# Spreading rows of norm scales by two small DMAs through memory instead of by matmuls, in a two-model float32 transformer kernel

## The chip, the cores and the metric

The kernel runs on one core of one Trainium2 chip, as one program of five engines that meet only at semaphores: TensorE (PE: matmuls and, beside them, weight loads), VectorE (DVE), ScalarE (ACT), GpSimd (POOL) and SyncE (SP, which issues most loads). 16 DMA engines move data between the chip's memory (HBM) and the on-chip SBUF. The metric is the device time of one run in microseconds (us), as the median of three runs.

## The reference

256 tokens of width 1024 go through three layers. Layer 0 has a mixer of sparse attention and pooling, layer 1 one of stick-breaking attention, layer 2 (a second model) one of retention and block-sparse attention; each mixer is followed by a feed-forward block (FFN). All is float32. Every mixer and every FFN starts with a norm of the rows, and this case is about what becomes of the rows' scales:

```python
def rms_norm(x, g):
    y = x32 * lax.rsqrt(jnp.mean(x32 * x32, axis=-1, keepdims=True) + EPS)
    return (y * g.astype(jnp.float32)).astype(x.dtype)

def swiglu(h, w1, w3, w2):
    return (jax.nn.silu(h @ w1) * (h @ w3)) @ w2

for layer in range(DEPTH):
    h = rms_norm(x, norm_mix_g[layer])
    x = x + mixer(h)
    h = rms_norm(x, norm_ffn_g[layer])
    x = x + swiglu(h, ffn_w1[layer], ffn_w3[layer], ffn_w2[layer])
```

## The kernel before

**Numbers.** Each float32 operand is split into a high part that PE takes as it is and a low part that holds the rest (ACT makes `high`, a subtraction on DVE makes `low`: lines 849/1399 for weights in the ring `raw`, 854/1405 for sums of weights in `arena`). A product takes three matmuls, high by high, high by low, low by high (L2149, L2150, L2154). PE is thus given a long, even row of matmuls, a unit of weights at a time, and DVE and ACT work some units ahead of it.

**Where scales go.** The x that PE multiplies (`xh`, `xl`) carries the norm's gain but not the row's scale: token p and token 128+p lie in partition p as `r0` and `r1` (`x_rstd(k, 0)`, `x_rstd(k, 1)`; k is the norm's number), and the products are scaled afterwards. POOL makes the scales in `row_rstd` (L764 and the power at L767), norm by norm, as the rows of x are finished.

**Who needs a row of them.** Some of the FFN's up-products, and the two gate products of layer 2's mixer, are made with seven products in place of eight, from sums of quarters of x and of the weights. These sums mix tokens p and 128+p, so the first half of x must first be brought to the second half's scale, by the ratio r0/r1 (`x_ratio`). x is transposed there, tokens along the free axis, so the 128 ratios are needed as a row, the same in all 128 partitions. Layer 1's mixer wants its q and k transposed and scaled by a row of all 256 scales. There are five such rows: norms 1, 3, 6 (the FFNs, f = 0, 1, 2), norm 4 (`mx_...`) and norm 2 (`o_rstd`).

**How PE spreads them.** DVE makes a matrix of ones, the reciprocal of r1, the ratio, and a diagonal matrix of the ratios (L1636 to L1641; L1936 to L1941 for norm 4; L1902 and L1904 for norm 2). PE multiplies ones by diagonal into a PSUM bank (`x_row_scales` L2389, L2873, `norm_rows` L2660; a float32 matmul shows as two pieces). In the FFN and the gates DVE reads that bank in the product of `x_sums` (L1594; L1947 for norm 4); for norm 2 ACT copies it to `o_rstd` (L1256), which `qk_scale` reads (L1913).

**Order.** Every engine's order is written out by hand. In an FFN, PE does two units of chunk 0, the small matmul, two units of chunk 1 with `hiddenT(0)` between them (transposes L2293, which wait for DVE's `gated(0, ...)`, L1540), `down(0)`, and then the first pair of seven products. DVE does the split of unit (1, 1), `x_sums` (L1594 to L1603), `gated(0, 1)`, `gated(0, 0)`, the first sum of weights (L1573), and goes on splitting. POOL, behind the scales of a norm, issues the load of the next norm's gains (`load_gain`, L753; after norm 1 first a table, L816), and in an FFN later four accumulating loads of weights (`weight_sums`, L798).

## Time and profile before

| | before |
|---|---|
| median of 3 runs | 951.77 us (951.42 to 952.23) |
| profiled execution: span from the first to the last instruction | 949.9 us |
| PE matmul busy | 942.9 us, 99% of the span |
| DVE / ACT / POOL busy | 795.1 / 578.5 / 80.7 us |
| granted TensorE clock | 1.00 throughout |

The span leaves out what lies around the instructions; the median is 1.9 us longer. Busy shares are means over the whole span: the page's table of 40 slices shows DVE at nine tenths or more in most slices of the three FFNs, and at five to eight tenths in many of those between them, while PE is at nine tenths or more in all but the first and the last.

### The profile page before, as it was taken

To read this page: it belongs to the slowest core of one execution; us is meant where nothing else is said; L and a number is where in the kernel's file an instruction comes from. 1 tells how busy PE (TensorE), PEld (TensorE's weight loads), DVE (VectorE), ACT (ScalarE), POOL (GpSimd) and SP (SyncE) were. 2 spreads that over 40 slices of the span, in tenths; PEclk is the share of its full clock that TensorE was granted. 3 is DMA by queue.
4 is the path that set the end of the run, shared out by engine and by line. 5 is a ranking of instruction groups with operands and counts; after the bars stand their busy time and mean duration, and the time that the engine had idled before them with its cause. 6 is when DMAs were issued, how large, how long until landed. Compare 5 with 4: busy or idle time off the path is not lost.

```text
span 949.9 us, 12049 instructions
## 1 busy us (share of the span) xinstructions
PE 942.9 (99%) x4719; PEld 786.6 (83%) x4719; DVE 795.1 (84%) x827; ACT 578.5 (61%) x611; POOL 80.7 (8%) x87
## 2 busy tenths in 40 slices
PE   8999999999999999999999999999999999999998
PEld 7878888888899888888888888888888888888887
DVE  5988999989866877999989887965885779999996
ACT  6566676576663655676666666565744456665672
POOL 3511101101000000101101021001010001101010
PEclk9999999999999999999999999999999999999999
DMA  8746888785464436879786365457255485987751
GB/s 303 263 134 210 245 305 226 203 284 133 153 223 136 155 112 220 244 252 258 199 280 163 116 219 182 171 182 218 93 198 196 164 275 139 318 236 208 256 133 45
DMA packets 125849, 191.14 MB, mean 201 GB/s; under 512 B 7256, under 2 KB 87520, under 8 KB 125792
## 3 DMA queue, kind: packets, MB, share of 16 engines
q1 hardware_dynamic: 110992, 172.59, 53.9%
q0 software_dynamic: 14496, 17.57, 10.5%
q8 instruction: 38, 0.62, 0.3%
q10 hardware_dynamic: 304, 0.20, 0.1%
q14 instruction: 19, 0.16, 0.0%
HBM read 189.29 MB, written 1.05 MB: 200 GB/s over the span
## 4 chain that ended last, share of the span: by engine, by line
PE 99%; DMA 0%; ACT 0%; issue 0%; DVE 0%; ACTq 0%
PE psum L2149 27%; PE psum L2150 26%; PE psum L2154 26%; PE psum L2293 4%; PE psum L2142 2%; PE psum L2144 2%; PE psum L2143 2%; PE psum L2684 1%; PE psum L2695 1%; PE psum L2685 1%; PE psum L2310 1%; PE psum L2718 1%; PE psum L2334 1%; PE psum L2746 1%; PE psum L2493 0%; DMA gains<-in_norm_mix_g 0%
## 5 line engine op out<-in xcount | busy, mean ns | idle before, releaser
L1399 DVE TENSOR_TENSOR low<-raw,high 128x2048 fp32r<-128x2048 f32 (+1 forms) x109 | 245.3, 2252 | 60.1 <-ACT high L849 60.1
L849 ACT ACTIVATE high<-raw 128x2048 fp32r<-128x2048 f32 (+1 forms) x112 | 211.6, 1890 | 83.8 <-PE psum L2154 69.1
L2149 PE MATMUL psum<-high,xh 128*128 128x512 f32 x596 | 237.1, 398 | 0.0
L2150 PE MATMUL psum<-high,xl 128*128 128x512 f32 x596 | 232.6, 390 | 0.0
L854 ACT ACTIVATE high<-arena 128x2048 fp32r<-128x2048 f32 x88 | 168.7, 1917 | 76.3 <-PE psum L2154 72.1
L1405 DVE TENSOR_TENSOR low<-arena,high 128x2048 fp32r<-128x2048 f32 x88 | 200.5, 2284 | 11.1 <-ACT high L854 11.1
L2154 PE MATMUL psum<-low,xh 128*128 128x512 f32 x596 | 155.4, 390 | 0.0
L2149 PEld LDWEIGHTS psum<-high,xh 128*128 128x128 f32 x596 | 112.0, 188 | 23.3 <-issue 0.7
L2154 PEld LDWEIGHTS psum<-low,xh 128*128 128x128 f32 x596 | 111.7, 188 | 23.6 <-issue 0.3
L2150 PEld LDWEIGHTS psum<-high,xl 128*128 128x128 f32 x596 | 112.0, 188 | 22.0
L2149 PE MATMUL psum<-high,mh 128*128 128x512 f32 x256 | 102.1, 399 | 0.0
L2150 PE MATMUL psum<-high,ml 128*128 128x512 f32 x256 | 99.9, 390 | 0.0
L2149 PE MATMUL psum<-high,gh 128*128 128x512 f32 x248 | 96.8, 390 | 0.0
L2150 PE MATMUL psum<-high,gl 128*128 128x512 f32 x248 | 96.5, 389 | 0.0
L2154 PE MATMUL psum<-low,mh 128*128 128x512 f32 x256 | 67.4, 389 | 0.0
L2154 PE MATMUL psum<-low,gh 128*128 128x512 f32 x248 | 61.5, 389 | 0.0
L2154 PEld LDWEIGHTS psum<-low,mh 128*128 128x128 f32 x256 | 48.1, 188 | 10.2
L2149 PEld LDWEIGHTS psum<-high,mh 128*128 128x128 f32 x256 | 48.1, 188 | 9.9 <-issue 0.3
L2150 PEld LDWEIGHTS psum<-high,ml 128*128 128x128 f32 x256 | 48.1, 188 | 9.4
L2154 PEld LDWEIGHTS psum<-low,gh 128*128 128x128 f32 x248 | 46.6, 188 | 9.7
L2149 PEld LDWEIGHTS psum<-high,gh 128*128 128x128 f32 x248 | 46.6, 188 | 9.6
L2150 PEld LDWEIGHTS psum<-high,gl 128*128 128x128 f32 x248 | 46.6, 188 | 9.6
(252 smaller groups left out, 1183.8 us busy)
## 6 DMA issues: line engine op xcount, KB each, us to landing
raw<-in_ffn_w SPq DMA_DIRECT2D x68, 512.0 KB, 6.5
arena<-in_ffn_w SPq DMA_DIRECT2D x64, 512.0 KB, 7.5
raw<-in_w_in SPq DMA_DIRECT2D x50, 512.0 KB, 4.6
raw<-in_od_w_qkv SPq DMA_DIRECT2D x24, 512.0 KB, 4.6
raw<-in_w_ffn_down SPq DMA_DIRECT2D x22, 512.0 KB, 6.4
arena<-in_ffn_w POOLq DMA_DIRECT2D x16, 512.0 KB, 7.5
arena<-in_w_ffn_gate SPq DMA_DIRECT2D x16, 512.0 KB, 6.5
arena<-in_w_ffn_up SPq DMA_DIRECT2D x16, 512.0 KB, 8.2
```

The lines of the kernel that those rows point to most:

```text
L849: nc.scalar.activation(high[:, n % RING, 0:cols], raw[:, r, 0:cols], ACT.Copy).then_inc(high_ready, 1)
L854: nc.scalar.activation(high[:, n % RING, :], src, ACT.Copy).then_inc(high_ready, 1)
L1399: nc.vector.tensor_tensor(low[:, n % RING, 0:cols], raw[:, RING_AT[n] % RING, 0:cols], high[:, n % RING, 0:cols].bitcast(F32), ALU.subtrac ...
L1405: nc.vector.tensor_tensor(low[:, n % RING, :], src, high[:, n % RING, :].bitcast(F32), ALU.subtract).then_inc(low_ready, 1)
L2142: nc.tensor.matmul(out, sh, wh, start=start, stop=False, skip_group_check=True)
L2143: nc.tensor.matmul(out, sh, wl, start=False, stop=False, skip_group_check=True)
L2144: return nc.tensor.matmul(out, sl, wh, start=False, stop=stop, skip_group_check=True)
L2149: nc.tensor.matmul(out, sh, wh, start=start, stop=False, skip_group_check=True)
L2150: nc.tensor.matmul(out, sl, wh, start=False, stop=False, skip_group_check=True)
L2154: return nc.tensor.matmul(out, sh, slot_tile(low, n, k, cols)[:, c0:c1], start=False, stop=stop, skip_group_check=True)
L2293: ins = nc.tensor.transpose(bank(dst_bank, j * P, (j + 1) * P), src, ident)
L2310: ins = nc.tensor.matmul(bank(lb[e], c0, c1), qT[rows, t * P:(t + 1) * P], kT[rows, 0:c1 - c0], start=t == 1, stop=masked and t == 0, skip ...
```

## The change

The row is no longer made by PE. POOL makes the ratio itself (`ratio_row`: the square root of the mean square by a power of 0.5, then r0 times that), issues a DMA that stores the 128 ratios (for norm 2 the 256 scales) as one line of a new tensor `rows_out` in the chip's memory, waits until it has landed, and issues a second DMA that loads this line into all 128 partitions (`spread_row`). DVE's `x_sums` reads the row from SBUF and waits for the second DMA (`ratio_row_in`, `rstd_row_in`) instead of for PE. The small matmuls, the ones, the diagonals, DVE's reciprocal and ratio, ACT's copy, and the waits that kept the PSUM banks free for them, are gone. POOL's loads of gains and of the table now stand behind the two small DMAs. The core of the diff:

```diff
+        rows_out = nc.dram_tensor("rows_out", (len(NORMS), SEQ), F32, kind="Internal").ap()
@@ POOL
+            nc.gpsimd.memset(pos_half, 0.5).then_inc(half_ready, 1)
+            def spread_row(k, src, dst, done):
+
+                i = ROW_NORMS.index(k)
+                row = rows_out[i, 0:src.shape[1] * P]
+                with nc.allow_non_contiguous_dma(reason="one value of each partition"):
+                    pool.dma_start(row.rearrange("(t p) -> p t", p=P), src).then_inc(row_stored, 16)
+                pool.wait_ge(row_stored, 16 * (i + 1))
+                pool.dma_start(dst, row.partition_broadcast(P)).then_inc(done, 16)
+
+            def ratio_row(k, dst):
+
+                nc.gpsimd.tensor_tensor(x_inv, msq[:, 2 * k + 1:2 * k + 2], pos_half, ALU.pow).then_inc(inv_made, 1)
+                pool.wait_ge(inv_made, ratio_seq(k))
+                pool.wait_ge(rstd_ready, 2 * NORMS.index(k) + 1)
+                nc.gpsimd.tensor_tensor(x_ratio, x_rstd(k, 0), x_inv, ALU.mult).then_inc(ratio_ready, 1)
+                pool.wait_ge(ratio_ready, ratio_seq(k))
+                spread_row(k, x_ratio, dst, ratio_row_in)
             for e in (1, 2, 3, 4):
                 row_rstd(e, e)
+                if e == 2:
+                    pool.wait_ge(rstd_ready, 6)
+                    spread_row(2, rstd[:, 4:6], o_rstd, rstd_row_in)
+                else:
+                    ratio_row(e, m_ratio if e == 4 else f_ratio)
@@ DVE, x_sums of an FFN
-                    dve.wait_ge(rbc_ready, f + 1)
+                    dve.wait_ge(ratio_row_in, 16 * ratio_seq(FFN_NORM[f]))
-                    nc.vector.tensor_tensor(f_x[:, :, 0:P], f_x[:, :, 0:P], bank(7, 0, P).unsqueeze(1).to_broadcast([P, KD, P]), ALU.mult
+                    nc.vector.tensor_tensor(f_x[:, :, 0:P], f_x[:, :, 0:P], f_ratio.unsqueeze(1).to_broadcast([P, KD, P]), ALU.mult
-                nc.vector.memset(f_ones, 1.0).then_inc(prep_step, 1)
-                nc.vector.reciprocal(x_inv, r1).then_inc(prep_step, 1)
-                nc.vector.tensor_tensor(x_ratio, r0, x_inv, ALU.mult).then_inc(prep_step, 1)
-                nc.vector.tensor_scalar(f_diag, ident, x_ratio, None, ALU.mult).then_inc(diag_ready, 1)
@@ PE, an FFN
-                x_row_scales()
+                pe.wait_ge(x_copied, 4 * f + 4)
@@ PE, layer 1's mixer
-                if u == 2:
-                    norm_rows()
@@ PE, layer 2's mixer
-                    nc.tensor.matmul(bank(5, 0, P), m_ones, m_diag, start=True, stop=True, skip_group_check=True).then_inc(mx_rbc, 1)
-                    if f == 0:
-                        pe.wait_ge(mx_step, 4)
```

On POOL, at the first FFN, the rows before run from the second scale of norm 1 to the table, the gains and the first accumulating load:

```order
L764 TENSOR_SCALAR small<-small 128x1 [waits sumsq_ready]
L767 TENSOR_TENSOR small<-small 128x1 [waits msq_ready]
L816 DMA cst<-consts 128x1536 [waits pooled_ready]
L753 DMA gains<-in_norm_mix_g 128x1024 [waits xn_ready]
L798 DMA arena<-in_ffn_w 128x4x256 [waits t_ready]
```

The same stretch of POOL in the changed kernel, where L774 and L777 are the scale, L791 and L794 the root and the ratio, L785 the store and L787 the load:

```order
L774 TENSOR_SCALAR small<-small 128x1 [waits sumsq_ready]
L777 TENSOR_TENSOR small<-small 128x1 [waits msq_ready]
L791 TENSOR_TENSOR small<-small 128x1
L794 TENSOR_TENSOR small<-small 128x1 [waits rstd_ready,inv_made]
L785 DMA rows_out<-small 128x1 [waits ratio_ready]
L787 DMA arena<-rows_out 128x128 [waits row_stored]
L849 DMA cst<-consts 128x1536 [waits pooled_ready]
L762 DMA gains<-in_norm_mix_g 128x1024 [waits xn_ready]
L826 DMA arena<-in_ffn_w 128x4x256 [waits t_ready]
```

Four rows came in between scale and table, two of them DMAs, and the load waits on POOL for the store. FFN 1 and FFN 2 read alike, without the table, and FFN 2 without the gains.

On DVE, in the first FFN, the rows before go from a split to `x_sums` and the two `gated` (L1399 are splits):

```order
L1399 TENSOR_TENSOR low<-raw,high 128x2048 [waits high_ready]
L1636 MEMSET arena 128x128 [waits rstd_ready]
L1637 RECIPROCAL small<-small 128x1
L1639 TENSOR_TENSOR small<-small 128x1 [waits prep_step]
L1641 TENSOR_SCALAR arena<-cst,small 128x128 [waits prep_step]
L1399 TENSOR_TENSOR low<-raw,high 128x2048 [waits high_ready]
L1594 TENSOR_TENSOR arena<-arena,psum 128x8x128 [waits x_copied,rbc_ready]
```

The same stretch of DVE in the changed kernel (L1431 are the splits, L1626 is the product of `x_sums`, L1572 the two `gated`):

```order
L1431 TENSOR_TENSOR low<-raw,high 128x2048 [waits high_ready]
L1431 TENSOR_TENSOR low<-raw,high 128x2048 [waits high_ready,rstd_ready]
L1626 TENSOR_TENSOR arena<-arena 128x8x128 [waits x_copied,ratio_row_in]
L1630 TENSOR_TENSOR arena<-arena 128x4x128 [waits prep_step]
L1631 TENSOR_TENSOR arena<-arena 128x4x128
L1633 TENSOR_TENSOR arena<-arena 128x4x128 [waits prep_step]
L1635 TENSOR_TENSOR arena<-arena 128x4x128 [waits prep_step]
L1572 SCALAR_TENSOR_TENSOR arena<-psum,small,arena 128x256 [waits silu_ready] x2
```

Four small instructions are gone ahead of the second split; the product of `x_sums` keeps its place and waits for the DMA's row.

## Rows read from the trace of the kernel before

**Rows 1.** The page: busy time by engine, and its chain by engine.

```profile
PE 942.9 (99%) x4719; PEld 786.6 (83%) x4719; DVE 795.1 (84%) x827; ACT 578.5 (61%) x611; POOL 80.7 (8%) x87
PE 99%; DMA 0%; ACT 0%; issue 0%; DVE 0%; ACTq 0%
```

**Rows 2.** All waits of PE: engine, line, releaser: us, times, longest.

```profile
PE psum L2499 <- DMA gains<-in_norm_mix_g: 4.2, 1, 4.2
```

**Rows 3.** Timeline of PE, first FFN: start us, us, engine, line, operation, tiles, count.

```profile
99.09 0.38 PE L2389 MATMUL psum<-arena 128*128 128x128 f32 x2
99.23 0.48 PE L2149 MATMUL psum<-high,xh 128*128 128x512 f32 x1
99.54 0.40 PE L2150 MATMUL psum<-high,xl 128*128 128x512 f32 x1
99.78 0.40 PE L2149 MATMUL psum<-high,xh 128*128 128x512 f32 x1
```

**Rows 4.** All pieces of L2389 and of L2873: ns min/median/max, first and last start.

```profile
L2389 PE MATMUL psum<-arena x6: 270/272/273, 99.1 to 783.7; 128*128 128x128 f32 x6
L2873 PE MATMUL psum<-arena x2: 270/272/273, 563.5 to 563.7; 128*128 128x128 f32 x2
```

**Rows 5.** Timeline of PE, layer 1's mixer, the row of norm 2.

```profile
275.18 0.60 PE L2660 MATMUL psum<-arena 128*128 128x128 f32 x4
275.54 0.36 PE L2684 MATMUL psum<-xh,high 128*128 128x256 f32 x1
275.74 0.28 PE L2685 MATMUL psum<-xl,high 128*128 128x256 f32 x1
275.86 0.28 PE L2684 MATMUL psum<-xh,high 128*128 128x256 f32 x1
```

**Rows 6.** Timeline of POOL, first FFN: the second scale of norm 1.

```profile
89.88 0.56 POOL L767 TENSOR_TENSOR small<-small 128x1 f32<-128x1 f32 x1
```

**Rows 7.** Timeline of DVE, first FFN: two splits, `x_sums`, the two `gated`.

```profile
89.98 2.28 DVE L1399 TENSOR_TENSOR low<-raw,high 128x2048 fp32r<-128x2048 f32 x1
...
92.78 2.28 DVE L1399 TENSOR_TENSOR low<-raw,high 128x2048 fp32r<-128x2048 f32 x1
...
99.51 1.22 DVE L1594 TENSOR_TENSOR arena<-arena,psum 128x1024 f32<-128x1024 f32 x1
...
103.43 0.87 DVE L1540 SCALAR_TENSOR_TENSOR arena<-psum,small,arena 128x256 f32<-128x256 f32 x2
```

**Rows 8.** Timeline of PE, first FFN: `hiddenT(0)`.

```profile
104.81 0.60 PE L2293 MATMUL psum<-cst,arena 128*128 128x128 f32 x4
```

**Rows 9.** Timeline of POOL, layer 2's mixer: an instruction alone and beside a split.

```profile
693.99 0.19 POOL L829 TENSOR_SCALAR small<-small 128x4 f32<-128x4 f32 x1 [39.19 <-DVE small L1983]
694.27 1.03 POOL L832 TENSOR_TENSOR small<-small 128x4 f32<-128x4 f32 x1
695.56 2.14 POOL L829 TENSOR_SCALAR small<-small 128x4 f32<-128x4 f32 x1 [0.27 <-DVE small L1983]
```

**Rows 10.** Timeline of DVE in the same stretch: the split.

```profile
695.39 2.26 DVE L1399 TENSOR_TENSOR low<-raw,high 128x2048 fp32r<-128x2048 f32 x1
```

**Rows 11.** Landing of POOL's gains load issued at 378.75 us (512 KB, L753).

```profile
DMA to landing us min/median/max: 3.9/3.9/3.9
```

**Rows 12.** Landing of POOL's eight loads of 0.2 KB near the start (L781).

```profile
DMA to landing us min/median/max: 5.1/5.7/5.8
```

**Rows 13.** Issues of the output's stores: engine, count, KB each, us to landing.

```profile
out<-xs SPq DMA_DIRECT2D x3, 256.0 KB, 2.0
```

**Rows 14.** A stretch of the first FFN: busy by engine, clock, DMA share, GB/s.

```profile
95.00:99.00 4.00, 4.00 (x19) 3.33 (x18) 2.45 (x6) 1.92 (x1) 0.00 (x0) 1.00 1.01 398
```

**Rows 15.** Timeline of DVE: first readers of norm 2's and of norm 4's row.

```profile
287.14 0.68 DVE L1913 TENSOR_TENSOR arena<-psum,arena 128x512 f32<-128x512 f32 x1
...
569.80 1.21 DVE L1947 TENSOR_TENSOR arena<-arena,psum 128x1024 f32<-128x1024 f32 x1
```

**Rows 16.** Timeline of POOL in layer 2's mixer: its next work behind norm 4.

```profile
564.01 3.30 POOL L774 TENSOR_TENSOR head_rs<-small 128x8 f32<-128x8 f32 x2 [8.56 <-DVE small L1485]
```

More of the change, by code:

```diff
@@ L287, in program @@
         gn_rstd = small[:, 238:246].rearrange("p (t h) -> p t h", t=NT)
+        pos_half = small[:, 190:191]
         x_ratio, x_inv = small[:, 254:255], small[:, 255:256]
@@ L320, in program @@
         f_s1 = take(512)
-        f_diag = take(P)
-        f_ones = take(P)
+        f_ratio = take(P)
         f_x = XT2.rearrange("p (k n) -> p k n", k=KD)
@@ L348, in program @@
         o_tok = blocks(take(NT * 512), NT)
-        o_ones, o_diag, o_rstd = take(P), blocks(take(SEQ), NT), take(SEQ)
+        o_rstd = take(SEQ)
         take.at = 4 * 512
@@ L372, in program @@
         r_kT = gate_b[:, 1, :].rearrange("p (j t) -> p j t", j=4)
-        m_ones, m_diag = arena[:, take.at:take.at + P], arena[:, take.at + P:take.at + 2 * P]
+        m_ratio = arena[:, take.at:take.at + P]
         r_v = blocks(take(NT * D), NT)
@@ L411, in program @@
         x_copied = sem("x_copied")
-        t_ready, t3_in, prep_step, rbc_ready = sem("t_ready"), sem("t3_in"), sem("prep_step"), sem("rbc_ready")
-        diag_ready = sem("diag_ready")
+        t_ready, t3_in, prep_step = sem("t_ready"), sem("t3_in"), sem("prep_step")
+        inv_made, ratio_ready = sem("inv_made"), sem("ratio_ready")
+        row_stored, ratio_row_in, rstd_row_in = sem("row_stored"), sem("ratio_row_in"), sem("rstd_row_in")
         sums_high, sums_low = sem("sums_high"), sem("sums_low")
@@ L556, in p2_unit, with ratio_seq @@
             return U_P2[0] + j + (3 if j >= 2 * P2_PAIR + 4 else 0)
+        RATIO_NORMS = (1, 3, 4, 6)
+        ROW_NORMS = sorted(RATIO_NORMS + (2,))
+        def ratio_seq(k):
+            return RATIO_NORMS.index(k) + 1
         def b12_block(p):
@@ L834, in _ @@
             row_rstd(6, 5)
+            ratio_row(6, f_ratio)
             weight_sums(2)
@@ L1253, in _ @@
                 chunk_half(1)
-                if u == 2:
-                    act.wait_ge(rbc_made, 1)
-                    nc.scalar.activation(o_rstd, bank(RBC_BANK, 0, SEQ), ACT.Copy).then_inc(rbc_copied, 1)
                 if u == Q_T_BEFORE:
@@ L1900, in _ @@
             nc.vector.memset(o_later.rearrange("p e (b n) -> p e b n", n=P)[:, :, 0:TRI // P:2, P - 1], 1.0).then_inc(ones_set, 1)
-            dve.wait_ge(rstd_ready, 6)
-            nc.vector.memset(o_ones, 1.0).then_inc(rdiag_ready, 1)
-            for t in range(NT):
-                nc.vector.tensor_scalar(o_diag[:, t, :], ident, x_rstd(2, t), None, ALU.mult).then_inc(rdiag_ready, 1)
             def qk_scale(half, f):
@@ L1935, in _ @@
             r0, r1 = x_rstd(4, 0), x_rstd(4, 1)
[L1936 to L1941 removed]
             def mx_sums():
[L1945 removed]
+                dve.wait_ge(ratio_row_in, 16 * ratio_seq(4))
                 dve.wait_ge(mx_copied, 4)
[L1947 removed]
+                nc.vector.tensor_tensor(m_x[:, :, 0:P], m_x[:, :, 0:P], m_ratio.unsqueeze(1).to_broadcast([P, KD, P]), ALU.mult
                                         ).then_inc(mx_step, 1)
                 a11, a12, a21, a22 = (m_x[:, 4 * q:4 * q + 4, t * P:(t + 1) * P] for t in range(NT) for q in range(2))
[L1950 removed]
+                dve.wait_ge(mx_step, 1)
                 nc.vector.tensor_tensor(a22, a21, a22, ALU.subtract).then_inc(mx_step, 1)
                 nc.vector.tensor_tensor(a21, a21, a11, ALU.subtract).then_inc(mx_step, 1)
[L1953 removed]
+                dve.wait_ge(mx_step, 3)
                 nc.vector.tensor_tensor(a11, a11, a22, ALU.subtract).then_inc(mx_step, 1)
[L1955 removed]
+                dve.wait_ge(mx_step, 4)
                 nc.vector.tensor_tensor(a12, a12, a11, ALU.subtract).then_inc(mx_step, 1)
@@ L2383, in sum_tile @@
                     return tile
-                def x_row_scales():
-                    pe.wait_ge(diag_ready, f + 1)
-                    pe.wait_ge(x_copied, 4 * f + 4)
-                    nc.tensor.matmul(bank(7, 0, P), f_ones, f_diag, start=True, stop=True,
-                                     skip_group_check=True).then_inc(rbc_ready, 1)
                 def product_1(p):
@@ L2654, in q_T @@
                     transposes(Q_T_BANK + t, [o_tok[:, t, j * P:(j + 1) * P] for j in range(4)], qkvT_ready)
-            def norm_rows():
-                pe.wait_ge(rdiag_ready, 1 + NT)
-                for t in range(NT):
-                    ins = nc.tensor.matmul(bank(RBC_BANK, t * P, (t + 1) * P), o_ones, o_diag[:, t, :], start=True, stop=True,
-                                           skip_group_check=True)
-                ins.then_inc(rbc_made, 1)
             def turned_unit(unit, second, mid):
@@ L2767, in _ @@
             for u in range(16):
-                if u == 2:
-                    norm_rows()
                 if u == Q_T_BEFORE:
```

41 lines of the change are left out of this document (13 added, 28 removed).

## The prediction, made before the change was run

> **What bounds the kernel now.** I read the page's busy times and its chain first: PE is at work for 942.9 of 949.9 us, and the chain that ended last is PE for 99% of its length [rows 1]. Then the table of waits with PE as the waiting engine: it has one row, 4.2 us at the very start [rows 2]. PE is never seen waiting again, so its row of matmuls is the time. Two things follow. Work taken off DVE, ACT or POOL is worth nothing here by itself: what hides it is PE. And a wait that PE does not have today costs its full length. The change takes a little off PE, and it puts a chain of two transfers in front of DVE work that PE soon needs. So the question is how long that chain is and how much room it has.
>
> The profiled span is 949.9 us and the median 951.77; I take differences from the span and add them to the median.
>
> **What PE loses.** In the first FFN the small matmul's two pieces start at 99.09, and the step from the next matmul to the one behind it is 99.23 to 99.54 [rows 3]. From 99.09 to 99.54 is 0.45 us; without the small one that is one ordinary step, 99.54 to 99.78, 0.24. So one such place is worth 0.21 us. The pieces of L2389 are six, two for each FFN, and L2873 has two [rows 4]: four places. The row of norm 2 takes 275.18 to 275.74, 0.56 us, against an ordinary step of 0.12 (275.74 to 275.86) [rows 5]: 0.44. Together 4 x 0.21 + 0.44 = 1.28 us, all of it on the path. That is the largest gain that I can find. DVE's four small instructions for each row, ACT's copy, and the PSUM waits stand beside a PE that does not wait for them: nothing. With one SBUF operand in place of a PSUM one, the product of `x_sums` is taken as unchanged.
>
> **What the new chain takes.** I follow the first FFN. The second scale ends at 89.88 + 0.56 = 90.44 [rows 6]; the square root could start there. But from 89.98 to 92.26 DVE runs a split, a subtraction of two SBUF tiles [rows 7]. What POOL does beside one is shown elsewhere: an instruction of 0.19 us at 693.99 took 2.14 us at 695.56 [rows 9], where a split ran from 695.39 to 697.65 [rows 10], and ended 0.05 us behind it. It was held until the split was through, with 0.19 - 0.05 = 0.14 us of it already done. So the root ends at 92.26 + 0.56 - 0.14 = 92.68. A dependent POOL instruction follows 0.09 us after (693.99 + 0.19 to 694.27) [rows 9]: the ratio is due at 92.77, and the next split starts at 92.78 [rows 7]. It is open which of them gets in first. The scale at 89.88 started 0.10 ahead of its split and kept its 0.56 us [rows 6, 7]; the instruction held at 695.56 was 0.17 behind. 0.01 ahead is nearer to the first, so I take it as not held: ratio done at 92.77 + 0.19 = 92.96 (the price of L829 alone), store issued at 93.05.
>
> The Trainium skill has this as a rule (SBUF — State Buffer, section "Who interferes with whom"): a VectorE instruction with two SBUF inputs contends with a GpSimd instruction that reads SBUF, and whichever starts second waits until the first is through. It speaks against moving the ratio to GpSimd at this place, and the row at 695.56 agrees with it. It does not say who wins a tie of 0.01 us.
>
> A store of 512 bytes and its load are not in the trace. From below: 2.0 us, a store of 256 KB from SP at the quiet end [rows 13]. From above: 5.8 us, the slowest of eight POOL loads of 0.2 KB beside a stream of weights [rows 12]. I take 3.9 us for each, POOL's gains load at 378.75 [rows 11]: it stands on the same queue, right behind the scales of FFN 1, where the store will stand. It is larger, but the stretch that the small ones fall into is fuller (DMA share 1.01, 398 GB/s from 95 to 99 [rows 14]), and the two should about cancel. Issue times lie inside landing times. Store 93.05 to 96.95, load 97.04 to 100.94, DVE at 101.03 with the same 0.09 for each hand-over. Before, `x_sums` started at 99.51 [rows 7]: it is 1.52 us late.
>
> The Trainium skill prices a GpSimd DMA at about 2.0 us plus bytes over 436 GB/s (DMA: Bandwidth & Descriptors, section "Anatomy of one DMA — SWDGE (gpsimd) path"). By that the two would take some 4.2 us, the row would be there by 97.4, and the time would be 950.5, the third case below. The eight small loads of this trace, at 5.1 to 5.8 us, do not bear this price out beside a full queue.
>
> **What lateness costs.** DVE is in order. Behind `x_sums` stand the two `gated`, which end at 103.43 + 0.87 = 104.30 [rows 7], and `hiddenT(0)` on PE, which needs them, starts at 104.81 [rows 8]. The room is 0.51 us. Behind PE's wait stand all its other products, so 1.52 - 0.51 = 1.01 us is lost in one FFN; the 0.21 that PE gained ahead of its wait is swallowed by it. Later consumers have more room or the same lateness, so nothing is added. FFN 1 and FFN 2 repeat the pattern with the same distances: three times.
>
> The other two rows have room. In the FFN the row comes 1.94 us behind the small matmul's place (101.03 against 99.09), or 4.1 if the ratio is held (a rival, below). Norm 4 has its small matmul at 563.5 [rows 4] and its row is first read at 569.80 [rows 15]. Norm 2 has its two at 275.18 [rows 5]; even issued only then, two transfers of 3.9 us would be through at 283.0, and its row is first read at 287.14 [rows 15]. POOL's own queue: the table and the gains, which could start at 90.44, now stand behind the load at 97.04, some 7 us later, and what follows them waits as well. The only near one is the power at 564.01 [rows 16]; by the FFN's distances the load of norm 4's row is issued at about 561.5, so POOL is about free by then, and I count nothing. The gains are wanted by the next norm and the accumulating loads by the pairs of products, so they cost nothing.
>
> **The forecast.** 3 x 1.01 lost, 0.44 + 0.21 kept (norms 2 and 4): +3.03 - 0.65 = +2.38. 951.77 + 2.38 = 954.2 us.
>
> **The rivals.**
>
> *The ratio is held too.* If the second split gets in first, the ratio ends 0.05 behind it, at 95.06 + 0.05 = 95.11. Store 95.20 to 99.10, load 99.19 to 103.09, DVE at 103.18: 3.67 late, 3.16 lost, three times 9.48. 9.48 - 0.65 = +8.8: 960.6 us. For it: 0.01 us is nothing to build on. Against it: the scale at 89.88.
>
> *The row is there in time* (the other side: not slower). It decides at the transfers: not held, DVE may start 0.51 - 0.21 = 0.30 late without any loss, so the two transfers may take 7.8 - 1.22 = 6.6 us together, 3.3 each. Then PE keeps the whole 1.28: 951.77 - 1.28 = 950.5 us. For it: the store is tiny and 2.0 is possible [rows 13]; the table and the gains, 1.25 MB in the first FFN, now queue behind the row and not beside it. Against it: the eight small loads [rows 12].
>
> *Something on PE that I don't see*, a bank or a wait that the small matmuls kept and that is worth over a microsecond: no wait of PE speaks for it [rows 2].
>
> The ends of the unknown prices: with 5.8 us for each transfer the first case gives 93.05 + 11.6 + 0.18 = 104.83, 5.32 late, 4.81 lost: +13.8, 965.6 us; held, 972.0. With 2.0 for each no case loses over 0.2 us.
>
> **How the numbers follow.** My forecast (late, ratio not held) 0.37; ratio held too 0.27; in time 0.33; unseen gain 0.03. A measurement of this kernel can tell about 0.2%, 1.9 us, from no change. The forecast's own spread, from 3.6 to 4.5 us a transfer, leaves about 0.08 of its chance within that; held gives nearly all to slower; in time is all but 0.02 within. So slower by over 0.2%: 0.55; within: 0.40; faster: 0.05. The range goes from the case in time, 950.5 with the run's own scatter, 950.2, to the held case with transfers of some 4.5 us (2 x 0.6 more in each of three FFNs, 3.6 in all: about 964): 950.2 to 964.0. Outside lie transfers near 5.8 and the unseen gain, under 2 in 10.
>
> **What would show it.** In the trace of the changed kernel: the duration of the root on POOL (about 2.3 us if held by the split) and of the ratio (0.2, or 2.3 if held); the landing times of store and load; DVE's wait for the row ahead of the product of `x_sums` in each FFN; and rows in PE's waits, three of them, at the transposes behind chunk 1. If PE's table of waits still has one row and the span is 1.3 us shorter, the row was in time and my price of the transfers was too high. If the waits are near 3 us each, the ratio was held. If the wait is at the row but at another place of PE, the room of 0.51 was wrong. If POOL's root is not held at all, the reading of rows 9 fails.

## The result, and the profile of the changed kernel

| | before | after |
|---|---|---|
| time, median of 5 runs | 952.17 us | 992.05 us (990.27 to 993.64) |
| profiled span | 949.9 us | 988.5 us |
| PE's share of the chain that ended last | 99% | 87% |

The ratio is 1.0423 (95% interval 1.0412 to 1.0435): 39.9 us slower, against a forecast of 954.2 us and a range that ended at 964. The span grew by 38.6 us.

The page of the changed kernel, busy times and the chain by engine, to be held against [rows 1]:

```profile
PE 948.9 (96%) x4707; PEld 789.5 (80%) x4707; DVE 793.0 (80%) x808; ACT 578.5 (59%) x610; POOL 98.7 (10%) x106
PE 87%; DMA 6%; POOL 2%; DVE 2%; issue 1%; ACT 1%; ACTq 0%; POOLq 0%; DVEq 0%
```

PE has fewer matmuls (4707) and yet more busy time, and transfers, which were not on the chain, now hold 6% of it. The table of waits (engine, line, releaser: us in total, times, longest) says who waits, where [rows 2] had one row for PE:

```profile
PE psum L2309 <- DVE arena L1572: 32.0, 3, 11.3
PE psum L2508 <- DMA gains<-in_norm_mix_g: 4.2, 1, 4.2
PE psum L2309 <- DVE arena L1522: 0.6, 2, 0.3
DVE arena L1626 <- DMA arena<-rows_out: 34.5, 3, 12.4
```

Three waits of PE at the transposes of `hiddenT(0)` (L2309) for the two gates of DVE (L1572), one in each FFN, and ahead of each a wait of DVE's product (L1626) for the row: the place that the prediction named, at ten times the length. GpSimd's timeline in the first FFN (start us, us, engine, line, operation; in brackets the idle time before and what ended it) answers to [rows 6]:

```profile
89.59 0.56 POOL L777 TENSOR_TENSOR small<-small 128x1 f32<-128x1 f32 x1
90.11 2.27 POOL L791 TENSOR_TENSOR small<-small 128x1 f32<-128x1 f32 x1
92.46 0.19 POOL L794 TENSOR_TENSOR small<-small 128x1 f32<-128x1 f32 x1
92.95 0.64 POOL L785 DMA_DIRECT2D rows_out<-small  x1 [0.30 <-POOL small L794]
103.93 0.54 POOL L787 DMA_DIRECT2D arena<-rows_out  x1 [10.34 <-DMA rows_out<-small]
```

The root (L791) takes 2.27 us, the ratio (L794) 0.19, the store is issued at 92.95 us where 93.05 was forecast. Up to there all went as foretold. Then GpSimd waits 10.34 us for a store of 512 bytes. The stores and the loads of all five norms, from issue to landing (view of one line, first L785, then L787):

```profile
DMA to landing us min/median/max: 10.0/10.7/10.7
```

```profile
DMA to landing us min/median/max: 5.2/6.1/8.0
```

What else happens while the store is under way is in the view of transfers from 93 to 104 us, in 40 slices (busy tenths of the 16 DMA engines, then GB/s):

```profile
DMA  2995999998999999999999966992949595972354
GB/s 56 246 220 216 369 410 372 372 432 343 417 380 324 335 373 366 377 388 380 302 182 153 112 112 138 104 108 86 112 175 130 123 104 93 97 101 75 97 108 108
```

From 98.5 us on the whole core moves about 100 GB/s and no longer 370, until the store lands at 103.65; weight loads of 512 KB issued in these 11 us take 11.7 and 14.4 us to land (medians of the two tensors), where in the kernel before those issued from 92 to 103 us took 10.3 and 8.3. The stores of norms 3, 4 and 6 show the same fall. At norm 2 little was under way, and the five weight loads issued there took 13.6 us where six in the kernel before, as close behind the norm (266 to 276 us), took 5.4. The time is not spent ahead of the store's packets. Queue 0, which carries them, in the views from 96.4 to 98.1 us and from 279.3 to 281 us:

```profile
q0 software_dynamic: 32, 0.00, 1.4%
q0 software_dynamic: 32, 0.00, 2.8%
```

These are all of the packets of the first store and of norm 2's; the views from there to the landings, 98.1 to 103.6 and 281.1 to 289.5 us, have no row of queue 0. So the first store lands more than 5 us behind its last packet, and norm 2's more than 8.

Where the time went is told by GpSimd's rows of the second scale of each norm, which stand at the same place in both kernels. Between them lie (us):

| stretch | before | after | difference |
|---|---|---|---|
| norm 1 to norm 2 (FFN 0) | 176.09 | 188.94 | +12.85 |
| norm 2 to norm 3 | 112.28 | 111.82 | -0.46 |
| norm 3 to norm 4 (FFN 1) | 176.09 | 189.28 | +13.19 |
| norm 4 to norm 6 | 220.09 | 220.81 | +0.72 |
| norm 6 to the end (FFN 2) | 175.75 | 188.33 | +12.58 |

The FFNs carry all of it, +38.6 us. In the first, `hiddenT(0)` comes 10.16 us later behind the scale (25.37 us after it, before 15.21), and from there to the next norm's first scale PE needs 161.81 us where it needed 159.11: 2.70 more, behind the wait. In the second FFN the two parts are 11.14 and 2.05 us, in the third 10.39 and 2.19.

The two small waits of PE (for L1522) stand behind norm 4. There VectorE scales the heads, and waits for a power on GpSimd that stood behind the store and the load (to be held against [rows 16]):

```profile
594.37 5.44 POOL L802 TENSOR_TENSOR head_rs<-small 128x8 f32<-128x8 f32 x2
```

It starts 15.01 us behind the second scale (579.36), where it started 9.95 behind it before (564.01 and 554.06).

### The profile page after: what moved, and what is told of

The parts are those of the page before. It is cut to its first block, busy times and chain, and to the rows that moved or that the text cites. A ratio compares the mean times of both kernels' runs of the same rounds, so it can differ in the third digit from the quotient of the medians.

```text
span 988.5 us, 12029 instructions
## 1 busy us (share of the span) xinstructions
PE 948.9 (96%) x4707; PEld 789.5 (80%) x4707; DVE 793.0 (80%) x808; ACT 578.5 (59%) x610; POOL 98.7 (10%) x106
## 3 DMA queue, kind: packets, MB, share of 16 engines
q0 software_dynamic: 14832, 17.97, 10.3%
## 4 chain that ended last, share of the span: by engine, by line
PE 87%; DMA 6%; POOL 2%; DVE 2%; issue 1%; ACT 1%; ACTq 0%; POOLq 0%; DVEq 0%
PE psum L2165 23%; PE psum L2166 23%; PE psum L2170 23%; DMA rows_out<-small 4%; PE psum L2309 4%; PE psum L2158 2%; PE psum L2160 2%; PE psum L2159 2%; DMA arena<-rows_out 2%; PE psum L2685 1%; PE psum L2696 1%; PE psum L2686 1%; POOL head_rs L802 1%; POOL small L791 1%; PE psum L2326 1%
## 5 line engine op out<-in xcount | busy, mean ns | idle before, releaser
L1431 DVE TENSOR_TENSOR low<-raw,high 128x2048 fp32r<-128x2048 f32 (+1 forms) x109 | 245.1, 2252 | 64.1 <-ACT high L883 64.1
L2165 PE MATMUL psum<-high,xh 128*128 128x512 f32 x596 | 239.8, 402 | 0.0
L2166 PE MATMUL psum<-high,xl 128*128 128x512 f32 x596 | 235.3, 395 | 0.0
```

What stands on the lines that cost most here:

```text
L1431: nc.vector.tensor_tensor(low[:, n % RING, 0:cols], raw[:, RING_AT[n] % RING, 0:cols], high[:, n % RING, 0:cols].bitcast(F32), ALU.subtrac ...
L2165: nc.tensor.matmul(out, sh, wh, start=start, stop=False, skip_group_check=True)
L2166: nc.tensor.matmul(out, sl, wh, start=False, stop=False, skip_group_check=True)
```

## Experiments

**The load without the store.** The store goes, the load reads gains of the norm, which lie in memory.

```diff
...
-pool.dma_start(row.rearrange("(t p) -> p t", p=P), src).then_inc(row_stored, 16)
-pool.wait_ge(row_stored, 16 * (i + 1))
-pool.dma_start(dst, row.partition_broadcast(P)).then_inc(done, 16)
+pool.dma_start(dst, NORM_G[k][0:src.shape[1] * P].partition_broadcast(P)).then_inc(done, 16)
```

> The changed kernel without its five stores: GpSimd loads the row, as soon as the ratio is made, from the first 128 (for norm 2, 256) gains of the norm, which lie in memory from the start. So the rows hold gains and not ratios, and nothing is waited for between ratio and load. Theory A (the store is the cause: it took 10.0 to 10.7 us from issue to landing, and the load behind it 5.2 to 8.0): the load is issued at about 92.7 us of the span in the first FFN and lands by 98.7, before VectorE is through with its split at 99.3, so PE does not wait for the FFN's rows and the time is that of before less the six small matmuls, 951.8 - 1.3 = 950.5 us. Theory B (whatever transfer GpSimd issues there first takes some 10 us, because the weight loads are ahead of it): the row lands at 103.5, VectorE is 4 us late in each of three FFNs, and the time is above 962 us.

Measured: 952.6 us, ratio 1.0011 (1.0002 to 1.0019). Without the store the loss is gone but for 1 us. The load by itself is dearer than I had it (its line's landing, then the waits of PE):

```profile
DMA to landing us min/median/max: 4.1/6.8/7.7
```

```profile
PE psum L2305 <- DVE arena L1568: 2.3, 3, 1.1
```

So even a store for nothing would have left PE waiting 2.3 us in all. Theory A holds for the store, not for its 950.5.

**The store without anyone who waits.** The kernel before, with five stores added behind the scales.

```diff
...
+pool.dma_start(rows_out[i, 0:n * P].rearrange("(t p) -> p t", p=P), rstd[:, 2 * k:2 * k + n]).then_inc(row_stored, 16)
```

> The kernel before, in which GpSimd also stores the column of norm scales (two columns for norm 2) to memory, 4 bytes from each partition, right behind the five norms at which the changed kernel does; nothing waits for a store but the end of GpSimd's program. Theory A (the store costs only whoever waits for it): PE and VectorE run as before, the time is 951.8 us within 0.5, the stores land after about 10.7 us. Theory C (the store also holds up other transfers: in the trace after, ScalarE waited 6.0 and 3.0 us for weights behind norm 2): weight loads issued in the 10 us behind each store land later than before, some of them too late, and the time is 953 to 960 us.

Measured: 958.27 us, ratio 1.0073 (1.0056 to 1.0090). Five stores that no engine waits for cost 6.7 us (the kernel before took 951.59 beside it). They landed somewhat sooner than in the changed kernel:

```profile
DMA to landing us min/median/max: 7.8/8.7/9.8
```

The rows of its table of waits that the kernel before did not have so, PE's, ScalarE's largest for transfers, and VectorE's largest (before 60.1 us, longest 4.5):

```profile
PE psum L2305 <- DVE arena L1959: 2.7, 1, 2.7
PE psum L2161 <- DVE gl L1559: 2.4, 1, 2.4
...
ACT high L861 <- DMA raw<-in_od_w_qkv: 12.5, 3, 8.2
ACT high L861 <- DMA raw<-in_ffn_w: 10.7, 3, 6.8
ACT high L861 <- DMA raw<-in_w_in: 7.2, 2, 6.4
...
DVE low L1411 <- ACT high L861: 70.4, 35, 12.2
```

ScalarE waits for weights, VectorE for ScalarE, PE for VectorE. Theory C: the store holds up the weight loads of another queue. Those issued from 91 to 101 us took 15.1 and 17.4 us to land, where the kernel before has 8.5 and 10.3. By the second scales the first FFN is 3.25 us longer and the stretch from norm 4 to norm 6 2.89; the other three stretches are as before.

**Five kinds of store.** Each norm stores in another way (a pair is the partitions and the words of each) and loads gains; the loads are alike.

```diff
+STORES = ("chip", (4, 32), "apart", (P, 16), (P, P))
...
+if kind == "chip":
+    pool.dma_start(row_sb[0:1, :].rearrange("o (p t) -> o p t", t=1), src).then_inc(row_stored, 16)
+elif kind == "apart":
+    pool.dma_start(wide_out[i, :, 0:1], src).then_inc(row_stored, 16)
+else:
+    n, w = kind
+    pool.dma_start(wide_out[i, 0:n, 0:w], ident[0:n, 0:w]).then_inc(row_stored, 16)
...
```

> The changed kernel with five kinds of store in the place of the one, each waited for as there; the row is then loaded from gains of the norm, so the rows hold gains and not ratios. Norm 1 (first FFN): 4 bytes from each of 128 partitions into one row of one partition of SBUF. Norm 2: 128 bytes from each of 4 partitions. Norm 3 (second FFN): 4 bytes from each partition, to places in memory 512 bytes apart. Norm 4: 64 bytes from each partition. Norm 6 (third FFN): 512 bytes from each partition, 64 KB in all. Theory A1 (the 4-byte element is what is slow, wherever it goes): 10 to 11 us for the first and third, 2 to 5 us for the other three. Theory A2 (128 writes into one piece of memory of 512 bytes are what is slow): 2 to 5 us for all but none of them 10, the first as well. Theory A3 (any store from that queue waits for something there): all five 10 to 11 us. By A1 the time is about 992 - 13 = 979 us, since only the third FFN's row comes some 7 us sooner; by A2 about 960; by A3 992.

Measured: 971.88 us, one run. The issues of the five, in the order of the program, from the views of transfers around them (tile, queue, count, KB, us to landing):

```profile
row_sb<-small POOLq DMA_DIRECT2D x1, 0.5 KB, 5.7
...
wide_out<-cst POOLq DMA_DIRECT2D x1, 0.5 KB, 1.7
...
wide_out<-small POOLq DMA_DIRECT2D x1, 0.5 KB, 5.6
...
wide_out<-cst POOLq DMA_DIRECT2D x1, 8.0 KB, 4.5
...
wide_out<-cst POOLq DMA_DIRECT2D x1, 64.0 KB, 5.7
```

No kind takes 10 us: not 4 bytes as such (first and third), not a store from that queue (fifth). And no stretch of 100 GB/s follows. GB/s from 388 to 395 us, where the third was under way from 388.51 to 394.1:

```profile
GB/s 0 0 0 70 47 257 164 211 304 304 328 328 374 421 398 445 421 421 398 398 363 299 287 287 310 340 352 370 386 380 387 387 375 398 386 380 374 386 451 328
```

A1 and A3 fall; A2 is nearer, though its landings came out at the upper end or above and its 960 us was too low: two transfers of 5 to 6 us are still too long.

**GpSimd's ratio with PE's rows.** The kernel before, with root and product on GpSimd; the rows are spread by PE.

```diff
...
-nc.vector.reciprocal(x_inv, r1).then_inc(prep_step, 1)
...
-nc.vector.tensor_tensor(x_ratio, r0, x_inv, ALU.mult).then_inc(prep_step, 1)
...
+dve.wait_ge(ratio_ready, ratio_seq(FFN_NORM[f]))
```

> The kernel before with one part of the change alone: GpSimd makes the ratio (root and product of one value in each partition), VectorE no longer does; the rows are still spread by PE's small matmuls from VectorE's diagonal, as before. Theory A (the transfers carry the whole loss): the ratio is there at 92.7 us, the diagonal at about 93, PE's small matmul comes at 99.09 as before; the time is 951.8 us within 0.5. Theory D (the ratio on GpSimd costs by itself, the root being held for 2.3 us behind VectorE's split): the diagonal comes late or VectorE's splits are held, and the time is 953 us or more.

Measured: 951.74 us, ratio 1.0002 (0.9993 to 1.0010). That part of the change costs nothing.

**The row on the chip.** The whole change, with the row held in one partition of SBUF and read from there 128 times.

```diff
-rows_out = nc.dram_tensor("rows_out", (len(NORMS), SEQ), F32, kind="Internal").ap()
+row_sb = sb("row_sb", [1, SEQ])
...
+pool.dma_start(row[:, t * P:(t + 1) * P].rearrange("o (p t) -> o p t", t=1), src[:, t:t + 1]).then_inc(row_stored, 16)
...
+pool.dma_start(dst, row.unsqueeze(1).to_broadcast([1, P, src.shape[1] * P])).then_inc(done, 16)
```

> The changed kernel with the row held on the chip: the store goes to 512 bytes of one partition of SBUF, 4 bytes from each partition (for norm 2 two such stores), and the load reads that one partition 128 times. In the run of five kinds of store such a store landed in 5.7 us and left the weight loads at 326 GB/s, where the store of the change landed in 10.7. Theory A2 (many 4-byte writes into one piece of memory are what is slow and what holds up the weights): store 5.7, load 4 to 6 us, the row in the first FFN in by 105 us, PE's wait there 5 to 6 us and not 11; the time is 972 us within 4, as with the five kinds. Theory A4 (whatever passes between one row and 128 partitions in small pieces is slow, on the way back too): the load takes 10 us, the row is in at 109 or later, and the time is above 985 us.

Measured: 972.55 us, ratio 1.0223 (1.0207 to 1.0239). Keeping the row on the chip is worth 992.05 - 972.55 = 19.5 us, half of the loss. In the first FFN the row is in 5.5 us sooner behind the scale: 5.0 of them are the store (5.7 us for 10.7), 0.5 the load (5.4 for 5.9). PE's waits are half as long, as theory A2 had them:

```profile
PE psum L2310 <- DVE arena L1573: 15.1, 3, 5.2
```

**PE kept at work in the wait.** The changed kernel, with matmuls that nobody reads.

```diff
+KEEP_WARM = 44
...
+for _ in range(KEEP_WARM):
+    nc.tensor.matmul(bank(7, 0, P), ident, ident, start=True, stop=True, skip_group_check=True)
 hiddenT(0)
```

> The changed kernel, in which PE does 44 matmuls of 128x128 on the identity, into a bank that nobody reads then, ahead of each wait for the first hidden block: some 9 us of work in a wait of 11. Nothing else moves, the row comes as late as before. Theory E (after each long wait PE works at half clock for a while: steps of 0.43 us where it was 0.23, granted clock 0.50, from 114.7 to 120.7 us in the first FFN): PE's waits shrink to 1 to 2 us each but end where they ended, the granted clock stays near 1.00, and the time falls by 2 to 2.8 us for each FFN, to 984 to 986 us. Rival F (PE is held by VectorE's splits and the weights after the wait, whatever its clock): 991 to 993 us.

Measured: 989.14 us, ratio 1.0394 (1.0369 to 1.0419). The gain of 2.9 us is less than expected. In the profiled execution (986.35 us) stores took up to 11.4 us and loads 6.2 to 7.1, so two of the waits ended later; the other three took 988.59 to 993.07 us at a mean granted clock of 0.997 to 0.998, so there the matmuls did not keep the clock up throughout. In the profiled one the stretch behind the wait is free of both. Windows of PE, first of the changed kernel, then of this one (stretch, us, PE busy, granted clock, DMA share, GB/s):

```profile
108.00:112.00 4.00, 0.00 (x0) 0.50 1.00 390
112.00:116.00 4.00, 1.31 (x5) 0.50 0.22 89
116.00:120.00 4.00, 4.00 (x11) 0.50 0.15 18
120.00:124.00 4.00, 4.00 (x19) 0.96 1.20 187
```

```profile
108.00:112.00 4.00, 4.00 (x38) 1.00 1.05 350
112.00:116.00 4.00, 2.90 (x26) 1.00 0.81 328
116.00:120.00 4.00, 3.27 (x17) 1.00 0.02 5
120.00:124.00 4.00, 4.00 (x19) 1.00 0.77 109
```

After a wait of 10 us in which PE did nothing it worked at 0.50 of its clock, 1.2 GHz, with 11 matmuls in 4 us and not 19; kept at work, it stayed at 2.4 GHz. From the end of the wait to the next norm's first scale this kernel takes 275.91 - 116.73 = 159.18 us, the changed one 161.81, the one before 159.11. So theory E holds. In the second FFN the same stretch is 159.17 us here, 161.16 in the changed kernel and 159.11 before; in the third, to the end, 160.63, 162.74 and 160.55. The clock is worth 2.6, 2.0 and 2.1 us, 6.7 us of the loss. A wait half as long does nearly the same: with the row on the chip PE waits 4.84 us in the first FFN, and from there to the next norm takes 271.70 - 109.94 = 161.76 us, 2.65 more than before; in the other two it is 1.70 and 1.74 more. After the waits of at most 1.1 us of the load without the store the granted clock stays at 1.00.

**The wait in another place.** The row on the chip, and on VectorE `x_sums` stands behind the gates. A later sum of weights and ScalarE's copy of the result, not shown here, come later as well.

```diff
 up(1, 1)
-x_sums()
 gated(0, 1)
 gated(0, 0)
 t1(2)
-down(0)
+x_sums()
 hiddenT(0)
+down(0)
...
```

> The kernel with the row on the chip and one more edit: on VectorE the step that waits for the row (x_sums) stands behind the two gates and the first weight sum of the FFN and no longer ahead of them, and ScalarE's copy of its result stands behind the first hidden block and the next gate. Theory G (the loss is the place of the wait: the gates that PE waits for stand behind it on VectorE): PE's wait at the first hidden block goes, the row (in at 105 us) is waited for by VectorE for about 1 us, and what is left is at most 1 to 2 us for each FFN by which VectorE's later splits come late; the time is 951 to 957 us. Rival H (the product is needed so soon that any row after 100 us costs its own lateness): 968 us or more.

Measured: 957.13 us, ratio 1.0057 (1.0042 to 1.0071): 15.4 us less, by order alone. VectorE at the row's landing, and all that PE waited for beside the start:

```profile
102.06 2.28 DVE L1606 TENSOR_TENSOR arena<-arena 128x2048 f32<-128x2048 f32 x1
104.62 1.23 DVE L1627 TENSOR_TENSOR arena<-arena 128x1024 f32<-128x1024 f32 x1 [0.29 <-DMA arena<-row_sb]
```

```profile
PE psum L2171 <- DVE low L1438: 4.6, 6, 1.1
```

The same row, as late as with the row on the chip, is now waited for 0.29 us (1.6 in the three FFNs together). The 15.4 us hold the clock too: PE has no wait longer than 1.1 us, and it stays at 1.00. Theory G.

**Steps in memory.** 4 bytes of each partition, at a distance given in words for norms 1, 2, 3, 4 and 6.

```diff
+STEPS = (16, 2, 32, 8, 64)
...
+spots = wide_out[i, 0:P * step].rearrange("(p s) -> p s", s=step)[:, 0:1]
+pool.dma_start(spots, src[:, 0:1]).then_inc(row_stored, 16)
...
```

> The changed kernel with 4 bytes stored from each of 128 partitions to places in memory that lie a step apart: 64 bytes at norm 1, 8 at norm 2, 128 at norm 3, 32 at norm 4, 256 at norm 6; the row is then loaded from gains of the norm, so the rows hold gains and not ratios. Next to each other (a step of 4) they took 10.0 to 10.7 us, 512 bytes apart 5.6. Theory A2 (writes that fall into one line of memory wait for one another): the time falls in a jump where the step reaches the line, say 10 us at 8 and 32 bytes and 5.7 at 64 and above; if the line is longer, the jump is later. Theory A5 (what counts is how much memory the 128 writes cover, so how many banks or channels serve them): the time falls step by step, from about 10 at 8 bytes over 8 at 64 to 6 at 256.

Measured: 972.13 us, one run. All five alike:

```profile
DMA to landing us min/median/max: 4.6/5.0/5.3
```

Neither a jump at 64 bytes nor a slope: between 4 bytes and 8 it is over, or so it looked.

**Shifted places.** As the last, with a step and a first word for each norm.

```diff
+STEPS = ((1, 0), (2, 8), (2, 0), (4, 8), (2, 8))
...
+spots = wide_out[i, first:first + P * step].rearrange("(p s) -> p s", s=step)[:, 0:1]
...
```

> The changed kernel with other places for the 4 bytes of each partition, each row of places in its own 64 KB of memory; the row is loaded from gains of the norm, so the rows hold gains and not ratios. Norm 1: next to each other, as in the change. Norm 2: 8 bytes apart, all shifted by 32 bytes. Norm 3: 8 bytes apart, not shifted. Norm 4: 16 bytes apart, shifted by 32. Norm 6: 8 bytes apart, shifted by 32. Known: 8 bytes apart, not shifted, took 5 us at norm 2; the packets of a store are of 32 bytes, so each of the 16 DMA engines carries 8 partitions. Theory L (two engines that write into one piece of 64 bytes wait for each other): norm 1 10.7 us; norm 3 5 to 5.7, since 8 values 8 bytes apart fill 64 bytes of their own; norms 2, 4 and 6, shifted so that pieces are shared, about 10. Theory M (only what is next to each other is slow): norm 1 10.7, the four others 5 to 5.7. Theory N (the place of the small tensor in memory is what was slow): all five 5 to 5.7.

Measured: 985.28 us, one run. The issues, norms 1, 2, 3, 4 and 6:

```profile
wide_out<-small POOLq DMA_DIRECT2D x1, 0.5 KB, 11.3
...
wide_out<-small POOLq DMA_DIRECT2D x1, 0.5 KB, 4.8
...
wide_out<-small POOLq DMA_DIRECT2D x1, 0.5 KB, 7.4
...
wide_out<-small POOLq DMA_DIRECT2D x1, 0.5 KB, 5.4
...
wide_out<-small POOLq DMA_DIRECT2D x1, 0.5 KB, 7.3
```

Theory N falls (another tensor, 11.3 all the same). L falls: shifted or not, 8 bytes apart make 7.3 and 7.4 in the FFNs, and norms 2 and 4, shifted, 5. M is nearly right, but 8 bytes apart in a full stretch is still 2 us dearer than the 5.0 to 5.6 us of 64 bytes and more in the FFNs (the last run and the one of five kinds), and weights are held up there: behind norm 6's store the loads of three weight tensors took 9.0, 10.7 and 12.3 us to land, in the last run, 256 bytes apart, 7.1, 8.4 and 10.0. So it is the distance. Where between 8 and 64 bytes it ceases to matter is not shown: 16 and 32 (5.4 and 4.9 us) were tried at norm 4 alone, where the changed kernel's store took 10.0. The second of these (4.8), and its like in the run before, 8 bytes apart at norm 2, stood where hardly a weight load was under way, which is why that run did not show it. Why close writes hold up the rest is not shown by these runs; it stays open.

**The change at two norms.** FFNs as before, norms 2 and 4 by the row on the chip.

```diff
-ROW_NORMS = sorted(RATIO_NORMS + (2,))
+ROW_NORMS = (2, 4)
...
```

> The change at norms 2 and 4 alone, with the row on the chip: the FFNs' rows are spread by PE's small matmul as before (the ratio is GpSimd's there too), norm 2's two rows and norm 4's one come by a store to one partition and a load from it. Theory A (those rows have room): two small matmuls of norm 2 and one of norm 4 leave PE, 0.44 + 0.21 = 0.65 us; the time is 951.7 - 0.65 = 951.1 us, within 0.4. Rival (the rows' transfers and the gains' load behind them delay something there): 951.7 us or more.

Measured: 951.4 us, ratio 0.9998 (0.9989 to 1.0006): not to be told from before. In the trace the gain can be seen. The second scales of norms 1 and 6 (start first), in this kernel and in the one before:

```profile
89.83 0.19 POOL L776 TENSOR_SCALAR small<-small 128x1 f32<-128x1 f32 x1 [0.93 <-ACT arena L926]
...
773.65 0.19 POOL L776 TENSOR_SCALAR small<-small 128x1 f32<-128x1 f32 x1 [0.94 <-ACT arena L926]
```

```profile
89.60 0.19 POOL L764 TENSOR_SCALAR small<-small 128x1 f32<-128x1 f32 x1 [0.93 <-ACT arena L888]
...
774.15 0.19 POOL L764 TENSOR_SCALAR small<-small 128x1 f32<-128x1 f32 x1 [0.94 <-ACT arena L888]
```

683.82 against 684.55: 0.73 us less, where 0.65 was expected. The start of the program (first load to norm 1) moves by as much from run to run, the second scale of norm 1 at 89.2 to 90.5 us in these traces, and hides it.

**Pairs of 8 bytes.** The store without anyone who waits, of two values of each partition side by side (the store's two operands, before and now).

```diff
-rows_out[i, 0:n * P].rearrange("(t p) -> p t", p=P), rstd[:, 2 * k:2 * k + n]
+rows_out[i, 0:2 * P].rearrange("(p t) -> p t", t=2), rstd[:, 2 * k:2 * k + 2]
```

> The kernel before with five stores that nobody waits for, as in the run of the store alone, but of both norm scales of a partition side by side: 8 bytes from each partition, 1 KB in all, in the place of 4. Theory L or M (the jam comes of 4-byte pieces next to each other, which share 64 bytes between engines): each store lands in about 5 us, the weights are not held up, the time is 951.7 us within 0.5 where the 4-byte stores gave 958.3. Rival (any store from the partitions holds up the weights): 956 us or more.

Measured: 951.65 us, ratio 1.0000 (0.9991 to 1.0009). Twice the bytes, half the time of the 4-byte stores to landing, and their 6.7 us are gone:

```profile
DMA to landing us min/median/max: 4.1/4.5/5.9
```

The weights are held up all the same, only less. Those issued from 91 to 101 us took 10.0 and 12.8 us to land (15.1 and 17.4 beside the 4-byte store, 8.5 and 10.3 before), and ScalarE's waits for the FFN's weights are 3.3 us (10.7, and 0.7 before). That much PE does not feel: it has no wait but the one at the start.

**VectorE's order mended.** As with the wait in another place, with three more steps moved.

```diff
 up(1, 1)
+t1(2)
 gated(0, 1)
 gated(0, 0)
-t1(2)
+down(0)
 x_sums()
 hiddenT(0)
-down(0)
-sums_lows()
 gated(1, 0)
 low_of(2, 1)
+sums_lows()
```

> The kernel with the row on the chip and the step that waits for it put later, with VectorE's order in each FFN mended where the last run showed PE waiting (4.6 us in six waits for VectorE's splits): the first weight sum stands ahead of the gates (its weights land by 92 us), the split of the down projection ahead of the step that waits, and the pair's first split and the gate ahead of the split of the sums. Theory G (nothing is left but the place of things on VectorE): VectorE has filled the time to the row's landing, its splits for the first pair are done 2 us sooner, PE waits for under 0.5 us in each FFN, and the time is that of before less the six small matmuls and what is left of the waits: 950.5 to 952 us. Rival (the transfers themselves still cost PE time through the weights): 954 us or more.

Measured: 952.11 us, ratio 1.0005 (0.9996 to 1.0014). All five rows come by transfers, PE has none of the small matmuls, and it waits for one thing more than before, 0.2 us:

```profile
PE psum L2171 <- DVE low L1438: 0.2, 1, 0.2
```

So the whole loss can be undone with the transfers kept; the change then is worth nothing, not the 1.28 us of the matmuls. By the second scales, the stretches of norms 2 and 4 are 0.49 and 0.27 us shorter than before, as they should be, but the three FFNs are 0.14, 0.17 and 0.30 longer where each should be 0.21 shorter. What takes these 0.4 to 0.5 us of an FFN is in the waits of the weight loads (PEld), in one row that the kernel before does not have:

```profile
PEld psum L2171 <- DVE low L1438: 2.1, 6, 0.6
```

PE reaches `hiddenT(0)` 0.28 us sooner behind the second scale than before, in all three FFNs (14.93 us for 15.21 in the first). It loses 0.42 to 0.58 us 22 to 25 us later, at these matmuls of low parts (127.10 and 129.95 us in the first FFN), whose splits VectorE now makes somewhat later: the one that starts 33.80 us behind the scale before (123.40) starts 34.61 behind it here (124.76). So what is left is VectorE's order again; whether another order gains it was not run.

## Why the prediction was wrong

The sign and the place were right, the size was not. By its own steps:

- **PE is the bound, and a new wait costs its length**: right. Three long new waits of PE, and the span grew by them and by what followed them.
- **The small matmuls are worth 0.21 us each and 0.44 at norm 2**: right for norms 2 and 4 together (0.73 measured for 0.65); in the FFNs it can be seen in the last run alone, where PE is at `hiddenT(0)` 0.28 us sooner, and is lost again behind it.
- **GpSimd's root is held by VectorE's split, the ratio is not**: right. 2.27 us and 0.19, at the place read from [rows 6, 7]; the store was issued 0.10 us before the forecast time. The rule of the Trainium skill (SBUF — State Buffer, "Who interferes with whom") agrees with that 2.27. The held-ratio rival did not come about.
- **Store and load 3.9 us each, 5.8 at most**: this is the step that failed. The store took 10.0 to 10.7 us and the load 5.2 to 8.0, so in the first FFN DVE's product came 10.33 us late where 1.52 was forecast, and even the case with 5.8 for each had 5.32. I priced the store by the nearest size and queue [rows 11, 12], all of them loads, or a store of 256 KB at the quiet end [rows 13]; no row wrote 4 bytes from each partition into adjacent places of memory, and the upper bound could not be had from loads. The five kinds show what the store would have cost in another form, 5.6 to 5.7 us in the FFNs, within my bounds but above the 3.9. The Trainium skill's price for such a transfer (DMA: Bandwidth & Descriptors, "Anatomy of one DMA — SWDGE (gpsimd) path", 2.0 us and next to nothing for the bytes) was further off: here 1.7 and 2.0 us were seen, for four pieces of 128 bytes and for a store to the chip at norm 2, both with the DMA engines idle; beside the weights no transfer of a row came under 4 us.
- **The room is 0.51 us**: right. DVE's product started those 10.33 us later (109.84 for 99.51), `hiddenT(0)` 9.88 (114.69 for 104.81): 0.45.
- **Nothing is lost behind the wait**: wrong. 2.70, 2.05 and 2.19 us in the three FFNs, and all but 0.1 us of each went when PE was kept at work: the clock.
- **The other rows have room**: right for norm 2 (-0.46 us), wrong for norm 4 (+0.72 where -0.21 was due). Its row was not waited for by PE; GpSimd's power behind it was, the one near thing on that queue [rows 16], which I counted as nothing with a store of 3.9 us. Behind a store of 10.0 GpSimd came to it 5.06 us later and was then held by a split of VectorE that was itself late for weights (5.44 us for the two, 3.30 in [rows 16]), and PE waited 0.6 us. With the row on the chip, whose store took 4.5 us there, the stretch is 219.81 us, 0.28 shorter than before, as it should be. That a transfer holds up the weights of the whole core, as in the run of the store alone, was in no case of mine.

The account closes: 12.85 + 13.19 + 12.58 for the FFNs, + 0.72 - 0.46 for norms 4 and 2, is +38.9, and -0.3 at the program's start, for the 38.6 us of the span. The FFNs are 10.16, 11.14 and 10.39 us of wait and 2.70, 2.05 and 2.19 behind it. In runs: the row through memory 19.5 us (to 972.55), the wait ahead of the gates 15.4 (to 957.13), VectorE's order behind them 5.0 (to 952.11); the clock's share lies in the first two.

## What to carry to other kernels

A value of each partition is not to be stored as adjacent 4-byte pieces of memory beside a stream of loads: a store of 8-byte pieces, or into one row on the chip, landed in about half the time, and the five stores of 8-byte pieces, though they held up weights for some 2 us, cost the kernel nothing. Two dependent transfers beside full queues are some 10 us even then, so what waits for them must stand behind the work that the bottleneck needs first, on an engine that goes in order. A transfer whose form has no row in the trace is not bounded by transfers of the other direction, and a wait of PE of 5 us or more is to be charged with the clock behind it, here 1.7 to 2.7 us each time.

## What the runs showed of the hardware that I had not expected

- A store of 512 bytes, 4 from each of 128 partitions to adjacent places in memory, landed in 9.5 to 11.4 us in the kernels that wait for it and in 7.8 to 9.8 where nobody does (norm 2's, of 1 KB, among them). In the first FFN of the changed kernel the core's traffic fell from some 370 to about 100 GB/s for 5 us of it, behind the store's own last packet. Nobody needs to wait: five such stores cost 6.7 us. 8 bytes apart it took 7.3 to 7.4 beside weight loads, 16 and more 4.9 to 5.6; 8-byte pieces side by side 4.1 to 5.9; 4-byte pieces into one row of SBUF 4.5 to 6.1.
- One partition of SBUF read 128 times by one transfer was no slower than a row of memory: 4.0 to 6.6 us against 5.2 to 8.0.
- After 5 us without a matmul as after 10, PE's next work ran at a granted clock of 0.50 (1.2 GHz); behind the waits of 5 us 1.70 to 2.65 us were lost, behind those of 10 2.05 to 2.70. After waits of at most 1.1 us the clock stayed at 1.00.
- A root on GpSimd that started 0.42 us behind a split of VectorE (90.11 against 89.69) was held to its end, and a product that started 0.03 us ahead of the next split (92.46 against 92.49) was not.
